# Three split passes for probabilities times values, a causal mask added on VectorE, one-at-a-time scatters, and five small reorderings, in a two-layer decoder trunk

## What is computed

```python
# attention, per head: 128 + 64 query/key channels, 128 value channels, 4 blocks of 128 queries
s = q_nope[:, q0:q1] @ k_nope[:, :q1].T + q_rope[:, q0:q1] @ k_rope[:, :q1].T   # einsum over heads
mask = jnp.arange(q0, q1)[:, None] >= jnp.arange(q1)[None, :]
s = jnp.where(mask, s, -jnp.inf)
p = jax.nn.softmax(s, axis=-1)
outs.append(p @ v[:, :q1])
# mixture of experts: the rows of each expert are collected, in blocks, before its three matmuls
xb = xf[buf_tok].reshape(n_blocks, MOE_BLOCK, D)
```

## Time and profile before

| | us |
|---|---|
| median of 3 runs | 1036.73 (1036.23 to 1038.21) |
| the profiled execution | 1036.58 |
| its span in the profile | 1034.6 |
| PE busy | 1018.2 (98%) |
| DVE busy | 588.7 (57%) |
| ACT busy | 449.8 (43%) |
| POOL busy | 69.6 (7%) |
| granted TensorE clock, mean | 0.995 of full |

### The profile page before, as it was taken

The page is one execution under the profiler, slowest core; times in us unless marked ns, Lnnn a source line. Parts: engine busy times, 40 slices in busy tenths (PEclk is TensorE's granted clock), DMA queues, the critical chain, the costliest instruction groups (busy, mean ns, idle before and its releaser), DMA issues.

```text
span 1034.6 us, 15267 instructions
## 1 busy us (share of the span) xinstructions
PE 1018.2 (98%) x5602; PEld 874.7 (85%) x5602; DVE 588.7 (57%) x808; ACT 449.8 (43%) x602; POOL 69.6 (7%) x137
## 2 busy tenths in 40 slices
PE   8999999999999999999999989999999999999997
PEld 7878887788888888888888889999988888888883
DVE  6676676254344444343436760010489888989886
ACT  6445554244142322222124410010567777877754
POOL 2200000000000001010000030000000000000041
PEclk9999999999999999999999999999999999999999
DMA  9021321535463627273624858696999999999996
GB/s 291 2 82 58 126 62 69 155 103 162 138 183 98 202 88 217 95 217 96 191 60 155 274 223 260 206 352 179 320 389 377 368 394 373 388 371 391 369 395 220
DMA packets 150012, 224.99 MB, mean 217 GB/s; under 512 B 16916, under 2 KB 97812, under 8 KB 149968
## 3 DMA queue, kind: packets, MB, share of 16 engines
q1 hardware_dynamic: 138464, 187.98, 54.2%
q0 software_dynamic: 10688, 35.87, 9.9%
q10 hardware_dynamic: 816, 0.54, 0.2%
HBM read 196.40 MB, written 29.02 MB: 218 GB/s over the span
## 4 chain that ended last, share of the span: by engine, by line
PE 87%; DVE 6%; DMA 3%; issue 2%; ACT 2%; POOL 0%; POOLq 0%; SPq 0%; DVEq 0%; ACTq 0%
PE bank L1231 22%; PE bank L1233 22%; PE bank L1232 21%; PE bank L1658 8%; PE bank L1682 4%; PE bank L1414 1%; DMA scratch<-ybuf,from_y 1%; PE bank L1243 1%; DVE w_lo L1853 1%; PE bank L1394 1%; PE bank L1405 1%; DMA ybuf<-n_y 1%; PE bank L1634 1%; PE bank L1553 1%; PE bank L1584 1%
## 5 line engine op out<-in xcount | busy, mean ns | idle before, releaser
L2335 DVE TENSOR_TENSOR u_lo<-u_raw,u_hi 128x2048 fp32r<-128x2048 f32 (+1 forms) x104 | 208.5, 2046 | 5.6 <-ACT u_hi L1077 5.5
L1077 ACT CAST u_hi<-u_raw 128x2048 fp32r<-128x2048 f32 (+1 forms) x104 | 177.8, 1723 | 51.2 <-DMA u_raw<-in_moe_w_up 21.0
L1231 PE MATMUL bank<-big_hi,w_lo 128*128 128x512 f32 (+1 forms) x368 | 136.5, 371 | 0.0
L1232 PE MATMUL bank<-big_lo,w_hi 128*128 128x512 f32 (+1 forms) x368 | 136.4, 371 | 0.0
L1233 PE MATMUL bank<-big_hi,w_hi 128*128 128x512 f32 (+1 forms) x368 | 136.4, 371 | 0.0
L1853 DVE TENSOR_TENSOR w_lo<-stage_own,w_hi 128x1024 fp32r<-128x1024 f32 (+1 forms) x89 | 103.3, 1207 | 11.9 <-ACT w_hi L825 11.8
L1231 PE MATMUL bank<-u_hi,nx_lo 128*128 128x512 f32 (+1 forms) x288 | 106.7, 371 | 0.0
L1014 ACT ACTIVATE scratch<-bank 128x512 f32<-128x512 f32 x21 | 12.5, 597 | 216.3 <-PE bank L1233 216.3
L1233 PE MATMUL bank<-u_hi,nx_hi 128*128 128x512 f32 (+1 forms) x288 | 104.5, 363 | 0.0
L1232 PE MATMUL bank<-u_lo,nx_hi 128*128 128x512 f32 (+1 forms) x288 | 104.4, 363 | 0.0
L2119 DVE TENSOR_TENSOR scratch<-scratch,bank 128x512 f32<-128x512 f32 x21 | 14.4, 687 | 150.8 <-ACT scratch L1014 150.8
(11 more groups left out here) (346 smaller groups left out, 1739.3 us busy)
## 6 DMA issues: line engine op xcount, KB each, us to landing
u_raw<-in_moe_w_gate SPq DMA_DIRECT2D x68, 512.0 KB, 6.7
u_raw<-in_moe_w_up SPq DMA_DIRECT2D x68, 512.0 KB, 7.8
u_raw<-in_moe_w_down SPq DMA_DIRECT2D x64, 512.0 KB, 10.6
stage_own<-in_ffn_w_gate SPq DMA_DIRECT2D x21, 512.0 KB, 6.0
stage_own<-in_ffn_w_up SPq DMA_DIRECT2D x21, 512.0 KB, 7.2
stage_own<-in_ffn_w_down SPq DMA_DIRECT2D x21, 512.0 KB, 4.6
xbuf<-scratch POOLq DMA_DIRECT2D x21, 496.0 KB, 5.7
u_raw<-in_moe_w_down SPq DMA_DIRECT2D x8, 1024.0 KB, 9.2
```

Of the source, the lines that this page charges most:

```text
L1077: s.copy(u_hi[u % HIS][0:rows, 0:size], u_raw[u % RAWS][0:rows, 0:size]).then_inc(n_hi, 1)
L1231: t_.matmul(dst, st_lo, mv_hi, start=start, stop=False, skip_group_check=check)
L1232: t_.matmul(dst, st_hi, mv_lo, start=False, stop=False, skip_group_check=check)
L2335: v.tensor_tensor(u_lo[u % RAWS][0:rows, 0:size], u_raw[u % RAWS][0:rows, 0:size], u_hi[u % HIS][0:rows, 0:size], ALU.subtract).then_inc(n ...
```

## The change

Eight edits, of which the first is the largest.

1. Probabilities times values becomes three split passes. ACT writes `probsT_hi` from all three banks (three copies, one semaphore step each), DVE writes `probsT_lo` as the difference; ACT writes `v_hi` and DVE `v_lo`. PE's four float32 matmuls per head become twelve float32r passes, of which the last four wait for DVE. ACT's new `v_out` stands ahead of the splits at the start of attention.
2. The mask is no longer added by PE. DVE adds it to the 128 diagonal columns of each score block in PSUM, waits for that add, and then finds the largest.
3. In the third pair of heads the `wo` splits stand at other places: (0), (1), (2, 3), (4) in place of (0), (1, 2), (3), (4, 5); in the last pair (5), (6, 7) in place of (6), (7).
4. `latents(0)` takes `norm_lo(2, 2)` inside it, ahead of the rotation of the shared key.
5. `rotate_q(0)` and `rotate_q(1)` take `latents_lo(2)` and `latents_lo(3)` inside them, between the product and its add.
6. In the first tiles of the dense SwiGLU the transposes of the last token block stand before the wait for the third weight tile, not behind it.
7. ACT copies the second rotated query one query block earlier (`q2_out(0, 1)`).
8. Each scatter waits until the one before has landed.

```diff
@@ POOL
             for c in range(2 * T):
+                if c:
+                    pool.wait_ge(scattered, 16 * c)
                 pool.indirect_dma_start(out=xbuf, out_offset=..., in_=xn[:, c % T, :], in_offset=None).then_inc(scattered, 16)
@@ ACT
+            def v_out(hd):
+                for b in range(2):
+                    last = s.copy(v_hi[:, 2 * b:2 * b + 2, hd * VD:(hd + 1) * VD],
+                                  bank[6 + b][:, :].rearrange("p (t h n) -> p t h n", t=2, h=2)[:, :, hd, :])
+                last.then_inc(v_high, 1)
...
-                    s.copy(probsT[:, 0:512], bank[0][:, :])
-                    s.copy(probsT[:, 896:1280], bank[2][:, 0:384]).then_inc(pT_act, 1)
+                    for b, (at, n) in enumerate(((0, 512), (512, 384), (896, 384))):
+                        s.copy(probsT_hi[:, at:at + n], bank[b][:, 0:n]).then_inc(pT_act, 1)
@@ PE
-                        for kr in (kr_lo, kr_hi):
-                            t_.matmul(dst[:, 0:n], q2[:, hd, tok(qb)], kr[:, 0:n], start=False, stop=False)
-                        t_.matmul(dst[:, tok(qb)], ident_b[:, :], causal[:, :], start=False, stop=True
+                        t_.matmul(dst[:, 0:n], q2[:, hd, tok(qb)], kr_lo[:, 0:n], start=False, stop=False)
+                        t_.matmul(dst[:, 0:n], q2[:, hd, tok(qb)], kr_hi[:, 0:n], start=False, stop=True
                                   ).then_inc(scores_done, 1)
...
+                    for kb, at in enumerate((0, 512, 896, 1152)):
+                        t_.matmul(bank[3][:, kb * P:S], v_lo[:, hd, kb, :], probsT_hi[:, at:at + S - kb * P],
+                                  start=kb == 0, stop=False)
+                        t_.matmul(bank[3][:, kb * P:S], v_hi[:, kb, own], probsT_hi[:, at:at + S - kb * P],
+                                  start=False, stop=False)
                     pe.wait_ge(pT_dve, pair * 2 + hd + 1)
-                        last = t_.matmul(bank[3][:, kb * P:S], v_nat[:, kb, hd * VD:(hd + 1) * VD],
-                                         probsT[:, at:at + S - kb * P], start=kb == 0, stop=kb == T - 1)
+                        last = t_.matmul(bank[3][:, kb * P:S], v_hi[:, kb, own], probsT_lo[hd][:, at:at + S - kb * P],
+                                         start=False, stop=kb == T - 1)
@@ DVE
                         dve.wait_ge(scores_done, pair * 8 + col + 1)
+                        own = bank[qb][:, qb * P:(qb + 1) * P]
+                        link(v.tensor_tensor(own, own, causal[:, :], ALU.add))
                         v.tensor_reduce(neg_max[:, col:col + 1], bank[qb][:, 0:(qb + 1) * P], AX.X, ALU.max, negate=True
```

More of the change, by code:

```diff
@@ L219, in trunk @@
         rotated = [over(f"rotated{t}", [P, H, 2, ROPE], "scratch", at) for t, at in enumerate((0, 1024, 3072, 4096))]
+        v_hi = over("v_hi", [P, T, 2 * VD], "scratch", 2048)
+        v_lo = over("v_lo", [P, 2, T, VD], "big_lo", 6 * S)
+        probsT_hi = over("probsT_hi", [P, 1280], "scratch", 7680)
+        probsT_lo = [over(f"probsT_lo{n}", [P, 1280], "scratch", 5120 + 1280 * n) for n in range(2)]
         kr_hi = over("kr_hi", [P, S], "krT")
@@ L652, in _ @@
             g.memset(eps_t[:, :], EPS).then_inc(eps_ready, 1)
[L653 to L658, removed]
+            link(g.memset(ident[:, :], 0.0))
+            g.affine_select(out=ident[:, :], in_=ident[:, :], compare_op=ALU.not_equal, fill=1.0, base=0,
+                            pattern=[[-1, P]], channel_multiplier=1).then_inc(consts_ready, 1)
             g.memset(causal[:, :], 0.0)
@@ L937, in exps @@
                     for qb in range(T):
-                        if pair == 0 and hd == 0 and qb == T - 1:
+                        if pair == 0 and hd == 0 and qb == T - 2:
                             q2_out(0, 1)
@@ L966, in attention @@
                 exps(1)
+                if more:
+                    act.wait_ge(v_done, pair + 2)
+                    v_out(0)
                 between(1)
@@ L975, in attention @@
                 head_out(1)
+                if more:
+                    v_out(1)
                 between(3)
@@ L987, in _ @@
                 attention(pair, True, next_pair(pair))
-            attention(H // 2 - 2, True, lambda place: [split("wo", k) for k in ((0,), (1, 2), (3,), (4, 5))[place]])
+            attention(H // 2 - 2, True, lambda place: [split("wo", k) for k in ((0,), (1,), (2, 3), (4,))[place]])
             act.wait_ge(k_done, H)
-            attention(H // 2 - 1, False, lambda place: [split("wo", k) for k in ((6,), (7,), (), ())[place]])
+            attention(H // 2 - 1, False, lambda place: [split("wo", k) for k in ((5,), (6, 7), (), ())[place]])
             def ffn_split(j):
@@ L1901, in latents @@
                                        ALU.mult, ALU.mult)
+                between()
                 kr = c[:, QR + KVR:DOWN]
@@ L1956, in _ @@
             dve.wait_ge(gainc_landed, 32)
-            latents(0)
-            norm_lo(2, 2)
+            latents(0, lambda: norm_lo(2, 2))
             norm_lo(3, 3)
@@ L1965, in _, with rotate_q @@
                 split(name, n)
-            def rotate_q(t):
+            def rotate_q(t, between=lambda: None):
                 dve.wait_ge(rope_done, t + 1)
@@ L2046, in turned @@
                 def turned(hd):
-                    dve.wait_ge(pT_done, pair * 2 + hd + 1)
-                    v.tensor_copy(probsT[:, 512:896], bank[1][:, 0:384]).then_inc(pT_dve, 1)
+                    for b, (at, n) in enumerate(((0, 512), (512, 384), (896, 384))):
+                        dve.wait_ge(pT_act, pair * 6 + (3 * hd + b + 1))
+                        last = v.tensor_tensor(probsT_lo[hd][:, at:at + n], bank[b][:, 0:n], probsT_hi[:, at:at + n], ALU.subtract)
+                    last.then_inc(pT_dve, 1)
                 def head_out(hd):
```

38 lines of the change are left out of this document (22 added, 16 removed).

## The result

The change makes the kernel faster: 1026.56 us median of 4 runs (1026.08 to 1027.43) against 1037.47 for the kernel before in the same session; the ratio is 0.9896, with a 95% interval of 0.9879 to 0.9913. The forecast was 1028.2. The profiled execution has a span of 1024.7 us, against 1034.6: 9.9 us less.

What follows compares the result with a forecast made beforehand. PE was taken as the bound, with 87% of the chain. From 1036.58 us, -3.8 - 0.8 + 0.5 + 0.8 + 0.7 - 0.3 - 0.5 - 5.0 = -8.4 gave 1028.2 us, range 1026.0 to 1035.0.

Steps and rivals of the forecast that it cites:

- Part 1: Attention: 32 masks leave PE at 0.12 us each, -3.8 us; DVE's add of 0.31 us is covered in usual heads.
- Part 2: Attention: three split passes replace one float32 matmul, 1.99 us against 2.08 a head, -0.8 us in all.
- Part 3: Attention's new waits: +0.5 us at the first head's fourth block, +0.8 and +0.7 at the seventh head.
- +0.8 and +0.7 at the seventh head: PE waits +0.8 us at the fourth block behind one more weight split, +0.7 at the transposes behind DVE's mask adds.
- Part 4: The other reorderings: -0.3 us for `norm_lo`, -0.5 for the transposes before the weight wait, 0 for the rest.
- `norm_lo`: `norm_lo(2, 2)` ahead of the key rotation brings forward what PE waited 0.59 us for: -0.3 us.
- First tiles: Transposes put before the weight wait fill a wait of 0.48 us with 0.85 us of work: -0.5 us.
- `rotate_q`: An earlier lo part trades against a later rotation on the same engine: 0, from -0.4 to +0.3 us.
- early copy of the rotated query: ACT's earlier copy of the second rotated query in attention: 0, with "the same goes for" as its reason.
- Part 5: Mixture's start: one scatter at a time removes PE's stall, -5.0 us (bounds 0 and -5.5), blaming scatters, not traffic.
- the loop's entry: Rival at the mixture's start: PE's entry into its job loop causes the stall, which stays; 1033.2 us, chance 0.30.
- late-scatter rival: Mixture: scatters land too late for the second job's rows, PE stands 9.4 us; 1037.6 us, chance 0.12.

Runs made afterwards that it cites:

- e9: Changed kernel with the output-projection (`wo`) splits of the third and last pairs moved to places chosen from idle times: 1024.43 us, ratio 0.9871.
- e6: Kernel before with only the mask moved from PE to a DVE add in PSUM: 1036.32 us, ratio 0.9983.
- e10: Changed kernel with ACT copying the second rotated query after the third exponential again, as before: 1028.35 us, ratio 0.9905.
- e7: Changed kernel with the output-projection (`wo`) splits back at their old places: 1027.91 us, ratio 0.9910.
- e1: Kernel before with only the scatter wait added, each scatter waiting for the one before to land: 1031.52 us, ratio 0.9937.
- e2: Changed kernel without the wait between scatters: 1033.39 us, ratio 0.9954.
- e4: Kernel before with the burst of eight scatters issued later, after PE has ended eight more groups of pieces: 1033.76 us, ratio 0.9961.
- e3: Changed kernel with scatters in pairs, a wait only ahead of every second one: 1026.93 us, ratio 0.9896.
- e12: Changed kernel with scatters in two bursts of four, one wait ahead of the fifth: 1026.23 us, ratio 0.9884.
- e5: Kernel before with only the split passes for probabilities times values: 1035.12 us, ratio 0.9975.
- e11: Changed kernel with the reorderings of `norm_lo(2, 2)`, `rotate_q` and the first dense SwiGLU tiles' transposes undone: 1028.17 us, ratio 0.9906.

## Why the prediction was right, point by point

**Part 1, mask off PE: -3.8, measured -3.6.** The add starts 0.33 us ahead of the search for the largest (e9's first two rows), 0.31 assumed, and no usual head waits. The price of 0.12 us a mask came out nearly right by some luck: it was read at the one place where a mask is worth only 0.07. There the pass behind it holds PE 0.17 us without a mask too, and not the 0.12 that the prediction expected to see; at the other three places a mask is worth 0.12 to 0.13. What the prediction did not see is that the mask alone is worth little: e6 kept 0.5 us of it in its ledger and 1.5 in the medians. Of the rest, edits 7 and 3 keep 1.26 and 0.7 us (e10, e7), since they hide waits that it makes.

**Part 2, split passes: -0.8, measured -1.7 to -1.8.** The term was mis-sized, inside its bounds. The twelve passes need 1.94 us and not 1.99, since a 128-column pass holds PE for 0.06 us (115.52 to 115.58) where the pass ahead of it has 256 columns. The rest is at the seams: the step from the rotated queries' transposes to the next head (115.90 to 118.41 before, 114.03 to 116.32 after) is 2.51 against 2.29. The float32 matmul was entered more slowly (0.43 us from the transposes' start to its own, against 0.35), and so was the pass behind it (118.41 to 118.56, against 116.32 to 116.43); I counted its span and not the seam. The estimate from the Trainium skill (FP8 and Floating Point Precision, TensorE Precision Notes: true float32 takes four passes) was 0.5 us a head; the traces have 0.22 to 0.25, nearer to the spacing of the rows.

**Part 3, new waits: +0.5 at the first head, measured 0.** The step that failed reads "PE's fourth block waits for it". It does not wait for that subtraction's end. Timelines of DVE and PE, after:

```profile
80.63 0.68 DVE L2006 SCALAR_TENSOR_TENSOR qn_lo<-bank,qn_hi 128x512 fp32r<-128x512 f32 x1
81.23 0.68 DVE L2011 TENSOR_TENSOR kn_lo<-bank,kn_hi 128x512 fp32r<-128x512 f32 x1
...
81.17 0.33 PE L1411 MATMUL bank<-kr_hi,q 128*128 128x384 f32 x1
81.35 0.39 PE L1248 MATMUL bank<-kn_hi,qn_lo 128*128 128x512 f32 x1
```

The block starts at 81.35, without a gap, while the subtraction runs until 81.91. In this one head `o_lo` is stepped by a semaphore instruction of its own that stands behind `kn_lo` in DVE's text, and not by an arithmetic instruction. The trace has that step (L2045) at 80.65, while `qn_lo` was still being computed and before the subtraction had even started (81.23). **+0.8 and +0.7 at the seventh head: measured 0.85 and 0.65.** DVE's difference ran until 155.20 + 0.68 = 155.88, and PE started at 155.94.

**Part 4.** `norm_lo`: -0.3, measured -0.27. First tiles: -0.5, measured -0.64. `rotate_q`: 0, measured 0. The early copy of the rotated query: counted as 0, and worth 1.26 us (e10). Against the kernel before the sum is the same, since no wait stood there; but the reason given ("the same goes for") was wrong: it guards against the mask's delay.

**Part 5: -5.0, measured -5.4.** The blame on the scatters and not on the loop's entry was right (e1, e2, e4); "the scatters and not traffic as such" as well (e3, e12). A rule of the Trainium skill stood against it (Runtime: NRT & Kernel Launch, Instruction fetch mechanics). The DMA queues of the kernel before in the stall, 609 to 618 us (packets, MB, share), hold the scatters' packets alone:

```profile
DMA packets 924, 3.33 MB, mean 370 GB/s; under 512 B 111, under 2 KB 111, under 8 KB 924
q0 software_dynamic: 924, 3.33, 94.3%
```

The trace records no instruction packet in it, and none in the gaps of e2, e4, e5 and e6 either, so nothing here shows a fetch as what held PE; the smooth loop entry of e1 and e4 speaks against it as well. The scatters were hidden, as forecast: issued until 641.48 (predicted landed 652, measured 646.8), read back by 658.0 (646.82 + 11.2), needed at 661.02. The cover was 3 us and not the 5 forecast, since the 666 at which PE was expected left out what parts 1 to 4 win ahead of it. The issues were 3.7 to 8.3 us apart, 4 to 7 expected. The late-scatter rival missed by these 3 us; in pairs the read is issued at 633.73 and the cover is far larger.

**The sum.** With the measured terms, -3.6 - 1.8 + 0.85 + 0.65 - 0.3 - 0.6 - 5.4 = -10.2 us, against -9.9 between the spans and -10.9 between the medians. In the ledger the 0.3 between the first two are 0.2 that come back between 60 and 80 us, in the stretch of edit 5 (e11 finds no more than 0.04 for that edit), and 0.1 net behind 740 us. The forecast of -8.4 was short by the split passes (1.0), the wait that never came (0.5) and the scatters (0.4), and had 0.2 too much for the masks. The range's lower end is a slip: part 2 at its lower bound of -3.8 gives 1028.2 - 3.0 = 1025.2, and not 1026.0.

**Where the 1.7 us at 743 went.** In the kernel before, 16 transposes of the last wide job run at the lower clock (3.43 us, clock 0.53 from 743.5 to 747), in the changed trace at the full one (1.92). It doesn't follow from the change: of the 14 traces of this study 4 have the slow form, among them e3, whose code before that point differs from the changed kernel's only in POOL's waits. The other three are of the kernel before, e4 and e5, so that the change makes it rarer (1 of 9 traces, against 3 of 5) is not excluded. Busy time by stretch, e3:

```profile
732.00:737.50 5.50, 5.50 (x32) 4.72 (x31) 3.86 (x4) 3.31 (x5) 0.00 (x0) 0.69 1.05 401
737.50:800.00 62.50, 62.50 (x304) 52.59 (x303) 54.79 (x40) 46.86 (x36) 2.93 (x4) 1.00 1.03 380
```

and the changed kernel:

```profile
732.00:737.50 5.50, 5.50 (x39) 4.90 (x38) 5.50 (x8) 4.94 (x6) 0.31 (x1) 1.00 1.04 400
737.50:800.00 62.50, 61.18 (x296) 50.75 (x294) 52.75 (x35) 44.71 (x35) 2.62 (x4) 1.00 1.04 379
```

e3 loses 1.7 us to the clock and then waits for nothing. The changed kernel keeps them and then stands still for 1.3 us (62.50 - 61.18). Both end within 0.1 us of each other. From here to 800 us the weights, at a DMA share of 1.03 to 1.05, set the pace, and what was won at 735 to 743 us was lost again, here and in e1. What was won earlier was kept there: e1's running difference is 5.2 us behind its scatters and 5.2 at 900 us.

**What stays open.** How a burst of eight scatters holds PE's instructions back. The runs show when: with eight back to back the gaps start 7.4 to 7.6 us after the first issue in four kernels, as the sixth issue ends, and 9.7 us after it in e4, and end 1.4 to 1.6 us behind the last; with two or four there are none. Five to seven in one burst were not tried.

## What to carry to other kernels

Where PE stops for no reason that the profile names, look at what another engine issues in a burst at that time, and break the burst: a wait every one, two or four transfers cost PE nothing here and gave 6 us. Move or undo small reorderings one at a time together with the main edit: a copy that looked worth nothing guarded 1.3 us, and the mask's move alone kept at most 1.5 of its 3.4. Put side work where an engine waits for another one's result, not where it merely isn't the bound.

## What the hardware showed that I had not expected

Eight indirect scatters issued 1.27 us apart held up PE's stream (gaps up to 1.04 us) and kept ACT waiting 7.15 us for a group of 32 pieces that PE had run by 611 us (in the changed trace ACT starts behind the 32nd piece). In the four kernels whose gaps came to 2.6 to 3.1 us in all, the granted clock right behind them was 0.50, the lower level, which cost 1.4 us in the kernel before and 3.0 us in e2; in e4, with gaps of 1.1 us, it stayed full. A semaphore step written as an instruction of its own went out at 80.65 us, while the arithmetic ahead of it on the same engine was still running (`qn_lo`, until 81.31) or had not begun (`kn_lo`, 81.23 to 81.91).
